# Splitting an expert's 3584 columns into steps of 1024, 1024, 768 and 768 instead of 1024, 1024, 1024 and 512

## What is computed

```python
def swiglu(h, w1, w3, w2):
    return (jax.nn.silu(h @ w1) * (h @ w3)) @ w2

def moe_swiglu(h, w_router, w1, w3, w2):
    logits = jnp.einsum('bsd,de->bse', h, w_router).astype(jnp.float32)
    top_val, top_idx = lax.top_k(logits, TOP_K)        # TOP_K = 2
    top_w = jax.nn.softmax(top_val, axis=-1)
    gates = jnp.sum(jax.nn.one_hot(top_idx, N_EXPERTS) * top_w[..., None], axis=-2)
    out = jnp.zeros_like(h)
    for e in range(N_EXPERTS):                         # 8
        out = out + gates[..., e:e + 1] * swiglu(h, w1[e], w3[e], w2[e])
    return out
```

## Time and profile before

| | |
|---|---|
| median of 3 runs | 1330.66 us (1330.33 to 1334.9) |
| profiled execution | 1333.77 us |
| its span, first to last instruction | 1332.3 us |
| TensorE busy | 1309.8 us (98%) |
| granted TensorE clock, mean | 0.983 |
| HBM read | 427.71 MB |
| ring DMAs | 672, 512 KB each |

### The profile page before, as it was taken

The page is one execution under the profiler, slowest core; times in us unless marked ns, Lnnn a source line. Parts: engine busy times, 40 slices in busy tenths (PEclk is TensorE's granted clock), DMA queues, the critical chain, the costliest instruction groups (busy, mean ns, idle before and its releaser), DMA issues.

```text
span 1332.3 us, 31085 instructions
## 1 busy us (share of the span) xinstructions
PE 1309.8 (98%) x13921; PEld 780.2 (59%) x13921; DVE 369.7 (28%) x497; ACT 245.9 (18%) x318; POOL 21.4 (2%) x37
## 2 busy tenths in 40 slices
PE   9999999999999999999999999999999999999995
PEld 6998888888998834543533643453363345346342
DVE  4767644435567420011110111001011000101102
ACT  5644533323663200000000000000000000000001
POOL 2000000000000000000000000000000000000000
PEclk9999999999999799999999999999999999999998
DMA  8825755513833979999999999999999999999994
GB/s 305 304 74 186 262 183 178 184 63 122 301 127 140 409 290 402 407 350 403 405 409 408 401 408 408 401 408 408 393 408 408 399 398 408 409 395 408 408 388 166
DMA packets 140266, 430.84 MB, mean 323 GB/s; under 512 B 12375, under 2 KB 18807, under 8 KB 140002
## 3 DMA queue, kind: packets, MB, share of 16 engines
q1 hardware_dynamic: 138546, 423.49, 82.4%
q0 software_dynamic: 1584, 5.33, 1.1%
HBM read 427.71 MB, written 2.11 MB: 323 GB/s over the span
## 4 chain that ended last, share of the span: by engine, by line
PE 95%; DMA 1%; DVE 1%; issue 1%; ACT 1%; SPq 0%; POOL 0%; POOLq 0%; DVEq 0%
PE psum L1813 39%; PE psum L1833 20%; PE psum L1350 9%; PE psum L1352 9%; PE psum L1351 9%; PE psum L1778 2%; PE psum L1566 1%; DMA ring<-in_moe_w 1%; PE psum L1867 1%; PE psum L1369 1%; PE psum L1855 0%; PE psum L1702 0%; PE psum L1525 0%; DMA x<-in_x 0%; PE psum L1422 0%
## 5 line engine op out<-in xcount | busy, mean ns | idle before, releaser
L1813 PE MATMUL psum<-ring,xe 128*32 128x512 f32 (+1 forms) x5632 | 537.6, 540 | 0.7 <-issue 0.7
L1813 PEld LDWEIGHTS psum<-ring,xe 128*32 128x32 f32 x5632 | 183.0, 110 | 334.4 <-issue 299.0
L1833 PE MATMUL psum<-ring,gT 128*32 128x256 f32 x4864 | 275.0, 385 | 0.9 <-DMA ring<-in_moe_w 0.9
L1833 PEld LDWEIGHTS psum<-ring,gT 128*32 128x32 f32 x4864 | 158.7, 112 | 120.1 <-issue 20.5
L1211 DVE TENSOR_TENSOR gate<-gate,psum 128x768 f32<-128x768 f32 (+3 forms) x32 | 25.5, 796 | 518.0 <-ACT gate L796 518.0
L882 DVE TENSOR_TENSOR wlo<-raw,whi 128x2048 fp32r<-128x2048 f32 (+1 forms) x66 | 145.2, 2227 | 56.0 <-ACT whi L628 56.0
L796 ACT ACTIVATE gate<-psum 128x768 f32<-128x768 f32 (+3 forms) x32 | 21.9, 684 | 606.4 <-PE psum L1813 606.4
L628 ACT CAST whi<-raw 128x2048 fp32r<-128x2048 f32 (+1 forms) x66 | 120.4, 1861 | 55.9 <-PE psum L1352 32.5
L1350 PE MATMUL psum<-whi,f_hi 128*128 128x512 f32 (+1 forms) x320 | 123.8, 387 | 1.9 <-DVE wlo L882 0.9
L1352 PE MATMUL psum<-whi,f_lo 128*128 128x512 f32 (+1 forms) x320 | 121.4, 379 | 0.0
L1351 PE MATMUL psum<-wlo,f_hi 128*128 128x512 f32 (+1 forms) x320 | 121.3, 379 | 0.0
(11 more groups left out here) (239 smaller groups left out, 833.5 us busy)
## 6 DMA issues: line engine op xcount, KB each, us to landing
ring<-in_moe_w SPq DMA_DIRECT2D x672, 512.0 KB, 13.5
raw<-in_ffn_w SPq DMA_DIRECT2D x33, 1024.0 KB, 5.6
raw<-in_w_mix_in SPq DMA_DIRECT2D x21, 1024.0 KB, 7.3
raw<-in_w_mix_out SPq DMA_DIRECT2D x8, 1024.0 KB, 5.1
raw<-in_w_mix_in SPq DMA_DIRECT2D x4, 544.0 KB, 7.2
x<-in_x SPq DMA_DIRECT2D x2, 512.0 KB, 4.7
raw<-in_w_mix_in SPq DMA_DIRECT2D x2, 512.0 KB, 6.7
bias_by_distance<-bias_once POOLq DMA_DIRECT2D x1, 1024.0 KB, 7.0
```

The costliest lines, as they stand in the source:

```text
L1813: ins = mm(banks(j, n)[o:o + 32, g, 0:2 * q].rearrange("p (i b c) -> p i b c", i=2, c=64), rows_[:, k * CAP + 32 * g:k * CAP + 32 * (g + 1 ...
L1833: ins = mm(bank[bk][32 * q:32 * (q + 1), at_:at_ + 256], gT[j % 2][:, a:a + 32], w[:, o:o + 256], start=j == 0 and n == 0 and at_ == 0, st ...
```

## The change

The third and the fourth step get 768 columns each, and their start is looked up in `FIRST`. Rows of `w1` and `w3` are 4 KB in steps 0 and 1 and 3 KB in steps 2 and 3. Each of the four up steps now takes 8 slots, and a slot of steps 2 and 3 holds 0.75 MB in two DMAs of 384 KB. The slots of down become 4 + 4 + 3 + 3. An expert has 46 slot uses, and the ring keeps 18 slots. VectorE's transposes of step 2 are made group by group, as those of step 3 were. The loops of the further sweeps are written out; they are not run here.

```diff
--- before.py
+++ after.py
@@ -47,11 +47,11 @@
-QUARTER = [256, 256, 256, 128]
+QUARTER = [256, 256, 192, 192]
+FIRST = [0, 256, 512, 704]
 STEPS = len(QUARTER)
 RING = 18
-RING_MORE = 14
-PER_EXPERT = 42
+PER_EXPERT = 46
@@ -449,26 +445,23 @@
             def load_up(f, who, turn, j, some=None):
 
-                nk = 1 if j < STEPS - 1 else 2
                 cols = 4 * QUARTER[j]
-                for b in some or range(KD // nk):
+                for b in some or range(KD):
                     to, until = free_slot(f + b, turn)
-                    to = to[:].rearrange("p (k i c) -> p k i c", k=nk, i=2)
                     for i, w in enumerate((moe_w1, moe_w3)):
                         src = w[0].rearrange("e (k p) c -> p e k c", p=P)
-                        src = src[:, ds(who, 1), nk * b:nk * (b + 1), 1024 * j:1024 * j + cols]
-                        sp.dma_start(to[:, :, i, :], src.rearrange("p e k c -> p (e k) c")
+                        src = src[:, ds(who, 1), b, 4 * FIRST[j]:4 * FIRST[j] + cols]
+                        sp.dma_start(to[:, cols * i:cols * (i + 1)], src.rearrange("p e c -> p (e c)")
                                      ).wait_op(moe_used, until, "sem-ge").then_inc(moe_full[ring_slot(f + b)], 16)
@@ -489,16 +482,16 @@
                 load_up(f + 24, who, turn, 3)
-                load_down(f + 28, who, turn, 2)
+                load_down(f + 32, who, turn, 2)
                 if last:
-                    load_down(f + 32, who, turn, 3)
+                    load_down(f + 35, who, turn, 3)
                     return
...
-                load_up(f + 32, then, turn, 0, range(0, 4))
-                load_down(f + 36, who, turn, 3)
-                load_up(f + 34, then, turn, 0, range(4, 8))
+                load_up(f + 35, then, turn, 0, range(0, 4))
+                load_down(f + 39, who, turn, 3)
+                load_up(f + 38, then, turn, 0, range(4, 8))
@@ -506,12 +499,8 @@
-                if sweep == 0:
-                    for e in range(1, EXPERTS - 1):
-                        expert(sweep, e, chosen_expert(e))
-                else:
-                    with sp.Fori(0, EXPERTS - 2) as e:
-                        expert(sweep, 1, chosen_expert(e + 1), turn=e)
+                for e in range(1, EXPERTS - 1):
+                    expert(sweep, e, chosen_expert(e))
@@ -1210,7 +1199,7 @@
-                for o, n in ((0, rows_ * q),) if j < STEPS - 1 else tuple((256 * g, q) for g in range(rows_)):
+                for o, n in ((0, rows_ * q),) if q == 256 else tuple((256 * g, q) for g in range(rows_)):
@@ -1898,25 +1883,25 @@
                 e_up(2, f + 12, turn, xe, range(0, 8), n)
                 e_down(sweep, 1, f + 20, e, turn, n)
-                e_up(3, f + 24, turn, xe, range(0, 4), n)
+                e_up(3, f + 24, turn, xe, range(0, 8), n)
                 pe.wait_ge(e_gT, STEPS * turn + (STEPS * (EXPERTS * sweep + e) + 3))
                 if not last:
                     gather(v + 1)
                 turn_places(v)
-                e_down(sweep, 2, f + 28, e, turn, n)
+                e_down(sweep, 2, f + 32, e, turn, n)
                 if last:
-                    last_down(sweep, f + 32, e)
+                    last_down(sweep, f + 35, e)
                     last_scatter(sweep)
```

More of the change, by code:

```diff
@@ L381, in ring_slot @@
         def ring_slot(f):
-            return f % RING if f < PER_SWEEP else (f - PER_SWEEP) % RING_MORE
+            return f % RING
         def fills(f):
[L387 to L390, removed]
+            return f // RING + 1
         def hidden(engine, c, t, i, turn):
@@ L451, in free_slot @@
                 slot = ring_slot(f)
-                if f < RING and slot < RAW_FIXED:
+                if f < RAW_FIXED:
                     sp.wait_ge(lo_ready, MOE0 - RAW_FIXED + slot + 1)
@@ L457, in free_slot @@
                     sp.wait_ge(go_ps, 4)
-                room = 1 if f < PER_SWEEP else 1 + RING - min(RING_MORE, PER_SWEEP % RING)
-                return ring[slot], sp.lower_val(PER_EXPERT * turn + (f + room))
+                return ring[slot], f + 1
             def load_up(f, who, turn, j, some=None):
-                nk = 1 if j < STEPS - 1 else 2
                 cols = 4 * QUARTER[j]
-                for b in some or range(KD // nk):
+                for b in some or range(KD):
                     to, until = free_slot(f + b, turn)
-                    to = to[:].rearrange("p (k i c) -> p k i c", k=nk, i=2)
                     for i, w in enumerate((moe_w1, moe_w3)):
                         src = w[0].rearrange("e (k p) c -> p e k c", p=P)
-                        src = src[:, ds(who, 1), nk * b:nk * (b + 1), 1024 * j:1024 * j + cols]
-                        sp.dma_start(to[:, :, i, :], src.rearrange("p e k c -> p (e k) c")
+                        src = src[:, ds(who, 1), b, 4 * FIRST[j]:4 * FIRST[j] + cols]
+                        sp.dma_start(to[:, cols * i:cols * (i + 1)], src.rearrange("p e c -> p (e c)")
                                      ).wait_op(moe_used, until, "sem-ge").then_inc(moe_full[ring_slot(f + b)], 16)
@@ L803, in expert @@
             def expert(sweep, e, turn=0, last=False):
-                for j, p in enumerate((-1, 7, 19, 27)):
+                for j, p in enumerate((-1, 7, 19, 31)):
                     silu(sweep, j, p, e, turn, groups(sweep, e))
@@ L1797, in arrived @@
             def arrived(f, turn):
-                pe.wait_ge(moe_full[ring_slot(f)], 96 * turn + 32 * fills(f))
+                pe.wait_ge(moe_full[ring_slot(f)], 32 * fills(f))
             def e_up(j, f, turn, rows_, some, n=GROUPS):
                 q = QUARTER[j]
[L1804 to L1812, removed]
-                                ins = mm(banks(j, n)[o:o + 32, g, 0:2 * q].rearrange("p (i b c) -> p i b c", i=2, c=64),
-                                         rows_[:, k * CAP + 32 * g:k * CAP + 32 * (g + 1)],
-                                         w[:, kk, :, :].rearrange("p i (b t c) -> p i b t c", t=4, c=64)[:, :, :, t, :],
-                                         start=k == 0, stop=k == KD - 1)
+                for k in some:
+                    w = ring[ring_slot(f + k)][:, 0:8 * q].rearrange("p (i b t c) -> p i b t c", i=2, t=4, c=64)
+                    arrived(f + k, turn)
+                    for g in range(n):
+                        for t in range(4):
+                            o = 32 * t
+                            ins = mm(banks(j, n)[o:o + 32, g, 0:2 * q].rearrange("p (i b c) -> p i b c", i=2, c=64),
+                                     rows_[:, k * CAP + 32 * g:k * CAP + 32 * (g + 1)], w[:, :, :, t, :],
+                                     start=k == 0, stop=k == KD - 1)
                     ins.then_inc(moe_used, 1)
@@ L1914, in expert @@
                     pe.wait_ge(pickT_sb, v + 1)
-                    e_up(0, f + 32, turn, xe, range(0, 4), then)
-                    e_down(sweep, 3, f + 36, e, turn, n)
-                    e_up(0, f + 34, turn, xe, range(4, 6), then)
+                    e_up(0, f + 35, turn, xe, range(0, 4), then)
+                    e_down(sweep, 3, f + 39, e, turn, n)
+                    e_up(0, f + 38, turn, xe, range(4, 6), then)
                     scatter(sweep, e, turn, v)
-                    e_up(0, f + 34, turn, xe, range(6, 8), then)
+                    e_up(0, f + 38, turn, xe, range(6, 8), then)
             def sweep_experts(sweep):
@@ L1927, in sweep_experts @@
                 pe.wait_ge(counts_sb, 1)
-                if sweep == 0:
-                    for e in range(EXPERTS - 1):
-                        expert(sweep, e)
-                else:
-                    with pe.Fori(0, EXPERTS - 1) as e:
-                        expert(sweep, 0, turn=e)
+                for e in range(EXPERTS - 1):
+                    expert(sweep, e)
                 expert(sweep, EXPERTS - 1, last=True)
```

6 lines of the change are left out of this document (3 added, 3 removed).

## The result

| | before | after |
|---|---|---|
| median, 10 runs each | 1332.74 us | 1340.22 us |
| lowest to highest | 1330.33 to 1334.9 | 1335.54 to 1342.54 |
| ratio, 95% interval | | 1.0057 (1.0044 to 1.0069) |
| span of the profiled execution | 1332.3 us | 1339.0 us |

The change made the kernel 7.5 us slower. The forecast was 4.8 us slower, 1335.5 us, with a range that holds the measured time. Of the 4.7 us between 1335.5 and 1340.22, 2.1 come from the kernel before, whose median is 1332.74 us from ten executions and was 1330.66 from the three that the forecast started from.

What follows compares the result with a forecast made beforehand. The prediction took the last weight block's landing, plus TensorE's work on it, to bound the kernel. Rows 0, additional DMAs 0.5, ring 2.6 and end 1.7 gave +4.8 us, median 1335.5 us, range 1328.5 to 1343 us.

Steps and rivals of the forecast that it cites:

- The bound: At the kernel's end: the last weight block's landing, plus TensorE's remaining work on it, sets the time.
- The rows: Ring loads: 736 rows for each engine per expert before and after, at 8.5 ns each beside bytes; 0 us.
- smaller transfers run slower: Rival, ring loads: DMAs of 384 KB fall to the 2 KB windows' rate, +7.8 us on top, 1343.3 us; 14%.
- 3 KB rows run as 4 KB rows: Rival, ring loads: short slots run at the 4 KB rate, -3.4 us on the rate, 1332 us; 11%.
- The additional DMAs: Ring loads: 64 more DMAs, 8 in each expert, each ending with a mark of its own; 0.5 us.
- The ring: First expert: short slots leave engines idle 8.2 us, less a covered gather pause of 5.6 us; net 2.6 us later.
- the 5.6: Gather of the first expert: the 5.6 us without a free slot would cost nothing, as work is queued on the engines.
- The end: last_down: 96 records in place of 64, with the same 1.8 us for the low clock; +1.7 us.
- The gather's cover: Copies to xe and VectorE's scatter selection, now covered by three slots of down(2), 5.3 us, not four; cost nothing.
- TensorE in the second expert: Rival: TensorE falls behind or waits there, its clock falls and it is late at the end; some 1340 us; 7%.

Runs made afterwards that it cites:

- first_new: The kernel before, but the first expert alone has the steps 1024, 1024, 768, 768; 1335.83 us, ratio 1.0029 to before.
- last_old: The changed kernel, but the last expert keeps the steps 1024, 1024, 1024, 512; 1338.13 us, ratio 1.0037 to the kernel before.
- first_old: The changed kernel, but the first expert keeps the steps 1024, 1024, 1024, 512; 1335.97 us, ratio 1.0019 to the kernel before.
- ends_old: The changed kernel, but the first and last experts keep the steps 1024, 1024, 1024, 512; 1331.54 us, ratio 0.9992 to the kernel before.
- before_by_arrival: The kernel before, but the first group of last_down takes each block as it lands; 1327.96 us, ratio 0.9973.
- ring_16: The kernel before with a ring of 16 slots in place of 18; 1337.07 us, ratio 1.0048.
- ring_17: The kernel before with a ring of 17 slots in place of 18; 1333.18 us, ratio 1.0008.
- down_8k: The kernel before, each down slot loaded by one 1 MB DMA with 8 KB rows in place of two of 512 KB with 4 KB rows; 1324.78 us, ratio 0.9949.
- even_odd: The kernel before, each ring DMA split in two, one for even and one for odd partitions; 1402.1 us in one execution.

## Why the prediction was right in direction and short in size

**The bound.** Right. The end hangs on the last landing: 6.2 of 6.7 us of the span are there already when `last_down` begins.

**The rows, 0 us.** Right, and by the right price. The number of rows did not change, six experts with the new steps cost -1.1 us (-2.7 to +0.5), and 3 KB slots came at 404, 404 and 395 GB/s where 401 was forecast. The price held beyond its two points: a row of 3 KB takes 126.1 ns where the line gives 126.0. The rival "smaller transfers run slower" needed 6.7 us in these six experts, and the interval excludes it. "3 KB rows run as 4 KB rows" needed 2.9 us less there, which the times and the two windows at 404 GB/s leave in doubt. But the row's duration is on the line and not below it, and in the traces the last DMA lands 0.9 us later, not 2.9 earlier.

**The additional DMAs, 0.5 us.** The right size for what they take of an engine: their marks are 64 rows of 4 bytes at 9.4 ns, 0.6 us. In the times it can't be told from nothing.

**Left out.** The 1.5 us that the program's last stretch is shorter wherever an expert has the new steps stand in no term. Without them the change would have cost some 9 us. That the sum came within 2.7 us of the measured loss is in part their doing, and so luck.

**The ring, 2.6 us.** The mechanism was right and the size off: it measured about 5 us (5.0 by the pairs of times, 5.1 by the landings). The term that was mis-sized is not the idle time but what comes back, the 5.6. By the rate rows the engines missed 12.9, 12.7 and 12.4 us in the first two windows with the new steps (the change, `first_new`, `last_old`), for the change 27 x (1 - 299/408) + 58 x (1 - 368/408). With the old steps it was 3.7, 5.1 and 4.7 us (before, `first_old`, `ends_old`). That is 8.1 us more, and 8.2 was forecast. In the third window the old steps missed 4.9, 3.2 and 3.3 us, which the new ones get back: 3.8, not 5.6. The net is 4.3 us by the windows, and the other 0.8 of the landings lies outside them. I had taken for the pause 3.9 us of the gather and 1.7 us by which down(2) was longer than up(3). The 1.7 us was this one execution's: down(2) took 12.25 us there, with the granted clock at 0.96 in that window, and 10.57 in the traces of `first_old`, `ends_old`, `before_by_arrival`, `ring_16` and `ring_17`, at 1.00. The gather alone, 3.9 us, would have given 4.3.

**The end, 1.7 us.** The size was right for this execution: `last_down` itself took 2.0 us more, and the pairs with and without it in the last expert differ by about 3.1 us. The lower clock is why it can't be had more exactly: it cost 0.2, 1.9, 2.1 and 3.0 us in four executions with two or three blocks. I had said both that TensorE waits longer ahead of it and that it still hardly waits. It waited 7.0 us there in the change and 6.3 in `first_old`, which both have the new steps in the last expert, against 3.8 in `last_old` and 3.2 in `ends_old`, `first_new` and before. `last_down` now waits for three landings in place of two, and a slot takes 2.57 us, which makes 5.8 us out of 3.2. The rest is not explained.

**The gather's cover.** Right. No wait of TensorE for `xe` appears behind the shorter down(2).

**TensorE in the second expert.** It did not become the bound; that rival needed TensorE late at the end, and it waited 7.0 us there.

## What to carry to other kernels

Price a change in row length by counting all rows before and after, not by the longer ones alone: here 736 stayed 736, and rows got longer only where that merged DMAs of neighbouring rows (`down_8k`, 112 rows fewer in each expert, 0.5% faster). A ring of equal slots loses what is left empty in them, but only where releases and not the engines set the pace, so look for the stretch with short times from issue to landing. Lay traces over each other at a point just ahead of the change before comparing them, and take a pause from more than one execution: the 3.9 us from the start and the 1.7 us of a lower clock were each as large as what was sought. Whatever is done behind the last landing counts in full, and is worth cutting to what truly needs the last block.

## What the runs showed of the hardware that I had not expected

Splitting a load of 128 partitions into a lower and an upper half, with the same rows, cut the rate from 408 to 244 GB/s while the engines stayed busy; even and odd partitions kept 375. A row's transfer took 88.5, 126.1, 163.5 and 316.6 ns at 2, 3, 4 and 8 KB, and a DMA's mark 9.4 ns. The queue of SyncE issued 8 DMAs in 5.32 us in `even_odd`, one in 0.67 us, so four DMAs for a slot come to more than the 2.57 us that the engines need for it. And the granted clock in the last 4 to 8 us differed between executions that did nearly the same: 0.50 through most of `last_down` in one, and 1.00 in another.
